# Cached keys stored channel-major, and a new division of state units and gate tiles over the two halves of the samples' attention

## What is computed

```python
def attention_sample(q, k, v, iq, ik, iw, rel_bias, cache_k, cache_v, cache_ik, page_table):
    rows = (page_table[:, :, None] * PAGE_SIZE + jnp.arange(PAGE_SIZE)[None, None, :]).reshape(DB, past)
    ik_all = jnp.concatenate([cache_ik.reshape(-1, IDX_DIM)[rows], ik], axis=1)
    idx = indexer_topk(iq, iw, ik_all, q_pos, n_sel)       # relu(iq . ik), weighed, top 256 of 1025
    ...                                                    # keys and values of the chosen positions
    return sparse_attention(q, k_sel, v_sel, q_pos, idx, rel_bias)

def ssd_recurrent(xs, dt, A, bm, cm, h0):                  # one step for each sample
    h = h * jnp.exp(dtt * A)[..., None, None] + jnp.einsum('bgr,bgrp,bgn->bgrpn', dtt, xt, bt)
    y = jnp.einsum('bgn,bgrpn->bgrp', ct, h)
```

## Time and profile before

| | us |
|---|---|
| median of 3 runs | 1402.03 (1401.03 to 1403.03) |
| the profiled execution, first to last instruction | 1401.1 |
| samples' attention | 354.9 to 498.4 |
| of it key half / softmax stretch / value half / tail | 76.0 / 10.8 / 46.0 / 10.7 |
| busy in the whole span: TensorE / VectorE / ScalarE / GpSimd | 1226.1 / 859.2 / 580.2 / 386.1 |

### The profile page before, as it was taken

How to read it: one execution, slowest core, us unless ns; L and a number is a source line. 1 busy time by engine, 2 the same in 40 slices (tenths; PEclk the granted TensorE clock), 3 DMA queues, 4 the chain that set the end, 5 groups by cost and what they waited for, 6 DMA issues and landing times.

```text
span 1401.1 us, 17183 instructions
## 1 busy us (share of the span) xinstructions
PE 1226.1 (88%) x4958; PEld 747.1 (53%) x4958; DVE 859.2 (61%) x2353; ACT 580.2 (41%) x1545; POOL 386.1 (28%) x510
## 2 busy tenths in 40 slices
PE   7998799999879989999899999877887877878786
PEld 6876477777656677678785553322232222222231
DVE  2055589998762347511248687789956767776543
ACT  1164458887654235300125434433343333333433
POOL 3220012213111200100023445433643334433341
PEclk9999899999999999989999999999999999999999
DMA  6563023324887821233369999999999999999995
GB/s 213 164 210 118 31 95 105 106 91 134 311 290 261 282 106 46 78 112 111 111 255 425 426 425 426 428 426 426 426 428 426 427 426 427 428 426 425 428 421 237
DMA packets 80473, 390.22 MB, mean 279 GB/s; under 512 B 13464, under 2 KB 23224, under 8 KB 44288
## 3 DMA queue, kind: packets, MB, share of 16 engines
q0 software_dynamic: 43104, 287.92, 49.5%
q1 hardware_dynamic: 34144, 92.68, 19.2%
q10 hardware_dynamic: 3136, 8.57, 1.7%
...
## 4 chain that ended last, share of the span: by engine, by line
DMA 25%; PE 16%; issue 3%; DVE 3%; ACT 2%; POOL 1%; POOLq 0%; DVEq 0%
DMA pe_uv<-d_uv,pe_idx 24%; PE pe_acc L1828 8%; PE pq_ps L1767 4%; PE pe_ph L1828 2%; POOL pe_uv L1951 1%; DMA pe_uv<-d_uv,pe_idxs 1%; DVE pe_uv L2090 1%; ACT pe_dg L1895 1%; ACT pe_w L1892 1%; DVE pe_tp L1994 1%; PE pe_ps L1786 0%; DVE pe_tv L1989 0%; ACT pe_gl L1889 0%; PE pe_pss L1786 0%; DVE pe_cand L2000 0%
## 5 line engine op out<-in xcount | busy, mean ns | idle before, releaser
L2090 DVE CUSTOM_DVE_ANT_0 pe_uv<-pe_uv,pe_hnat 128x1024 f32<-128x1024 f32 x264 | 322.8, 1223 | 186.2 <-DMA pe_uv<-d_uv,pe_idx 171.3
L1951 POOL DMA_INDIRECT pe_uv<-d_uv,pe_idx x256 | 271.9, 1062 | 382.5 <-PE pe_ph L1828 177.7
L1828 PE MATMUL pe_ph<-pe_uv,pe_dg 128*128 128x512 f32 x512 | 252.7, 617 | 65.2 <-ACT pe_dg L1895 65.2
L1828 PE MATMUL pe_acc<-pe_uv,pe_dg 128*128 128x512 f32 (+1 forms) x544 | 257.2, 611 | 45.2 <-ACT pe_dg L1895 45.2
L1828 PEld LDWEIGHTS pe_ph<-pe_uv,pe_dg 128*128 128x128 f32 x512 | 86.9, 189 | 230.3 <-ACT pe_dg L1895 167.8
L139 PE MATMUL pi_ps<-xn,pi_w 128*128 128x264 f32 x848 | 203.4, 395 | 3.1 <-DVE xn L350 3.1
L1889 ACT ACTIVATE pe_gl<-pe_a 128x1 f32<-128x1 f32 x264 | 53.4, 202 | 366.6 <-DVE pe_a L2090 366.4
L1828 PEld LDWEIGHTS pe_acc<-pe_uv,pe_dg 128*128 128x128 f32 (+1 forms) x544 | 94.3, 185 | 199.6 <-ACT pe_dg L1895 110.7
L139 PEld LDWEIGHTS pi_ps<-xn,pi_w 128*128 128x128 f32 x848 | 162.1, 195 | 31.3 <-issue 4.4
L1895 ACT ACTIVATE pe_dg<-cst,pe_w 128x128 f32<-128x128 f32 x256 | 102.7, 401 | 8.3
L1892 ACT ACTIVATE pe_w<-pe_gl,pe_gw 128x1 f32<-128x1 f32 x256 | 75.4, 295 | 8.3
...
## 6 DMA issues: line engine op xcount, KB each, us to landing
...
ss_h<-d_state SPq DMA_DIRECT2D x8, 1024.0 KB, 7.5
o_ssm_s<-ss_h SPq DMA_DIRECT2D x8, 1024.0 KB, 9.5
...
paged<-d_ck POOLq DMA_DIRECT2D x40, 128.0 KB, 5.0
paged<-d_cv POOLq DMA_DIRECT2D x32, 128.0 KB, 5.1
```

Source lines behind the costliest of these rows:

```text
L1828: mm = pe.matmul(accs[n][0:m, 4 * half:4 * half + 4, :], lhsT, uv[:, r, D_MODEL + half * 512:D_MODEL + (half + 1) * 512], start=False, sto ...
L1951: pool.indirect_dma_start(uv[:, r, :], None, k.d_uv[:], bass.IndirectOffsetOnAxis(ap=src, axis=0)).then_inc(gathered[r], 16)
L2090: dve.tensor_tensor_reduce(uv[:, r, 0:D_MODEL], uv[:, r, 0:D_MODEL], hnat[:, n, :], 1.0, 0.0, ALU.mult, ALU.add, a[:, r:r + 1]).then_inc(d ...
```

## The change

The host stores the cached keys and indexer keys channel-major: channels on the partitions, positions along the row. An indexer page is then 64 rows of 512 bytes and goes to the upper or the lower 64 partitions, two pages side by side; a key page is as before 128 rows of 1 KB. The transposes and the copies of both stages go, with the tiles `cs_ikt`, `as_kt` and `cs_tr` (`cs_px` is left of it), and the products read `paged` itself. The ring's loads now wait for the products of a visit (`logits`) where they waited for its transposes. In the new listing the changed lines stand some 15 to 27 lines higher.

The work beside the two halves is divided anew: 8 units and 8 gate tiles in the key half (12 and 4 before), 8 units and 5 gate tiles in the value half's steps (4 and 9 before); the two gate tiles in the softmax stretch and the last one remain. SP's queue starts with state and gate weights in turns, and the stores and reloads stand at other visits.

```diff
@@ -48,7 +48,7 @@
 FIRST0 = N_ATT + 1
 GATE0 = FIRST0 + N_Z + N_XBC
-N_LAST, N_KEYS = 16, 4
+N_LAST, N_KEYS = 16, 8
 COLUMNS = "z" * 8 + "x" * 4 + "z" * 2 + "x" * 28 + "z" * 6
@@ -58,7 +58,7 @@
 Q0, K0, V0, IQ0 = 0, 8, 10, 12
 IW_P, DT_P = 64, 96
 WSLOTS, BANKS = 4, 2
-IK_FIRST, IK_SECOND = 36, 50
+IK_FIRST, IK_SECOND, IK_PAIRS = 18, 25, TS * PAGES // 2
 KV_SLOTS, KV_PAGES = 4, 4
@@ -247,11 +247,12 @@
 def load_indexer_pages(eng, k, first, end, loaded):
-    ik = k.paged[:].rearrange("p (a d) -> p a d", d=HD)
+    ik = k.paged[:].rearrange("p (a s) -> p a s", s=PG)
     with eng.Fori(first, end) as i:
-        page = eng.value_load(k.pages[0:1, bass.ds(i, 1)], min_val=0, max_val=k.n_pool - 1)
-        eng.dma_start(ik[:, bass.ds(i, 1), :], k.d_cik[bass.ds(page, 1)].rearrange("a s d -> s a d")
-                      ).then_inc(loaded, 16)
+        for odd in range(2):
+            page = eng.value_load(k.pages[0:1, bass.ds(i * 2 + odd, 1)], min_val=0, max_val=k.n_pool - 1)
+            eng.dma_start(ik[odd * HD:(odd + 1) * HD, bass.ds(i, 1), :],
+                          k.d_cik[bass.ds(page, 1)].rearrange("a d s -> d a s")).then_inc(loaded, 16)
 def project_attention(nc, k):
@@ -535,33 +537,23 @@
                       ).then_inc(spread, 1)
             k.proj.multiply(pe, tail[0])
-            pe.wait_ge(k.ik_loaded, 16 * (TS * PAGES - IK_SECOND + IK_FIRST))
-            pe.wait_ge(k.ik_by_sp, 16 * (IK_SECOND - IK_FIRST))
+            pe.wait_ge(k.ik_loaded, 32 * (IK_PAIRS - IK_SECOND + IK_FIRST))
+            pe.wait_ge(k.ik_by_sp, 32 * (IK_SECOND - IK_FIRST))
             def scores(b):
-                pe.wait_ge(copied, b + 1)
                 for half in range(2):
                     hd = slice(half * HD, half * HD + HD)
-                    pe.matmul(ps[0:TS * IH, half, :], iqd[hd, b, :], ikt[hd, b % 2, :],
+                    pe.matmul(ps[0:TS * IH, half, :], iqd[hd, b, :],
+                              ik[hd, b * (PAGES // 2):(b + 1) * (PAGES // 2), :].rearrange("p a s -> p (a s)"),
                               start=b == 0, stop=b == TS - 1)
                 pe.matmul(ps[0:TS * IH, 2, 0:1], iqd[0:HD, b, :], k.misc[0:HD, TP + b:TP + b + 1],
                           start=b == 0, stop=b == TS - 1).then_inc(scored, 1)
-            for b in range(TS + 1):
-                if b < TS:
-                    if b >= 2:
-                        pe.wait_ge(copied, b - 1)
-                    for j in range(PAGES // 2):
-                        at = b * PAGES + 2 * j
-                        mm = pe.transpose(tr[:, b % 2, j * P:(j + 1) * P],
-                                          ik[:, at:at + 2, :].rearrange("p a d -> p (a d)"), k.ident)
-                    mm.then_inc(turned, 1)
-                if b == 1:
-                    pe.wait_ge(diag, TS)
-                if b:
-                    scores(b - 1)
-                if b == 5:
+            pe.wait_ge(diag, TS)
+            for b in range(TS):
+                scores(b)
+                if b == 4:
                     pe.wait_ge(s_weighed, 2)
                     pe.wait_ge(dA_ready, 1)
@@ -595,17 +587,10 @@
             act.wait_ge(k.steps_loaded, 48)
             act.activation(alog, alog, ACT.Exp).then_inc(alog_ready, 1)
             k.proj.evacuate(act, tail[0])
-            for b in range(TS):
-                act.wait_ge(turned, b + 1)
-                if b >= 2:
-                    act.wait_ge(scored, b - 1)
-                act.activation(ikt[:, b % 2, :], tr[:, b % 2, :], ACT.Copy).then_inc(copied, 1)
-                if b == 1:
-                    act.wait_ge(u_ready, 1)
-                    act.activation(l, u, ACT.Ln).then_inc(log_ready, 1)
-                if b == 4:
-                    act.wait_ge(dA_ready, 1)
-                    act.activation(both[rows, TS:2 * TS], k.dA[rows, NP_:ALL], ACT.Exp).then_inc(both_dA, 1)
+            act.wait_ge(u_ready, 1)
+            act.activation(l, u, ACT.Ln).then_inc(log_ready, 1)
+            act.wait_ge(dA_ready, 1)
+            act.activation(both[rows, TS:2 * TS], k.dA[rows, NP_:ALL], ACT.Exp).then_inc(both_dA, 1)
             act.wait_ge(scored, TS)
             for half in range(2):
@@ -1341,12 +1325,12 @@
...
-        EARLY = 12
+        EARLY = 8
...
@@ -1355,15 +1339,16 @@
         VK = PAGES * TS // GP
-        after = ([[(t - 3) // 3] if t % 3 == 0 and 3 <= t < 3 + 3 * N_KEYS else [] for t in range(VK)]
+        after = ([[t // 2] if t % 2 == 1 else [] for t in range(VK)]
                  + [[N_KEYS, N_KEYS + 1]] + shares(range(N_KEYS + 2, N_LAST - 1), TS))
+        unit_at = {2 * u: u for u in range(EARLY)}
         spans = ((0, 512), (512, 512), (PAST, 1))
         def load(eng, loaded, half, visit):
             if visit < VK + NG:
-                eng.wait_ge(turned, 2 * (visit - NG + 1))
+                eng.wait_ge(logits, visit - NG + 1)
             elif visit >= VK + NG:
                 eng.wait_ge(mixed, visit - VK - NG + 1)
@@ -1388,16 +1373,16 @@
         def _(sp):
             for b in range(ssd.SLOTS):
                 ssd.load(sp, b)
-            store_at = {6 + 2 * b: b for b in range(6)} | {24: 6, 28: 7}
-            load_at = {7 + 2 * i: ssd.SLOTS + i for i in range(TS - ssd.SLOTS)}
+                gates.load(sp, b)
+            store_at = {8: 0, 12: 1, 16: 2, 19: 3, 24: 4, 28: 5, 31: 6}
+            load_at = {9: 3, 13: 4, 17: 5, 20: 6, 25: 7}
             for visit in range(NG, 2 * VK):
                 load(sp, by_sp, 0, visit)
                 if visit in store_at:
                     ssd.store(sp, store_at[visit])
                 if visit in load_at:
                     ssd.load(sp, load_at[visit])
-                if visit - NG < gates.SLOTS:
-                    gates.load(sp, visit - NG)
+            ssd.store(sp, TS - 1)
             ssd.all_stored(sp)
         @block.gpsimd
@@ -1416,37 +1401,25 @@
             def products(visit):
                 page = visit // 2
-                pe.wait_ge(copied, 2 * visit + 2)
+                arrived(pe, visit)
                 for j in range(2):
                     for i in range(GP):
                         rows = slice(32 * i, 32 * i + 32)
                         mm = pe.matmul(pl[rows, page // 4, page % 4 * P:(page % 4 + 1) * P],
                                        qd[:, 2 * i + visit % 2, j, :],
-                                       kt[:, (2 * visit + i // 2) % 4, (2 * (i % 2) + j) * P:(2 * (i % 2) + j + 1) * P],
+                                       kv[:, visit % NG, i, j * P:(j + 1) * P],
                                        start=False, stop=False, tile_position=(0, 32 * i))
                 mm.then_inc(logits, 1)
-            for n in range(4 * PAGES + 2):
-                if n < 4 * PAGES:
-                    visit = n // 2
-                    if n % 2 == 0:
-                        arrived(pe, visit)
-                    if n >= 2:
-                        pe.wait_ge(copied, n - 1)
-                    for i in range(2):
-                        for j in range(2):
-                            mm = pe.transpose(tr[:, n % 2, (2 * i + j) * P:(2 * i + j + 1) * P],
-                                              kv[:, visit % NG, 2 * (n % 2) + i, j * P:(j + 1) * P], k.ident)
-                    mm.then_inc(turned, 1)
-                if n % 2 == 0 and 0 <= n // 2 - 1 < EARLY:
-                    ssd.spread_c(pe, n // 2 - 1)
-                if n % 2 == 1 and n >= 3:
-                    products(n // 2 - 1)
-                if n % 2 == 1 and n // 2 < VK:
-                    for g in after[n // 2]:
-                        gates.multiply(pe, g)
-                if n % 2 == 1 and n // 2 < EARLY:
-                    ssd.spread_b(pe, n // 2)
+            ssd.spread_b(pe, 0)
+            for visit in range(VK):
+                products(visit)
+                if visit in unit_at:
+                    ssd.spread_c(pe, unit_at[visit])
+                for g in after[visit]:
+                    gates.multiply(pe, g)
+                if visit + 1 in unit_at:
+                    ssd.spread_b(pe, unit_at[visit + 1])
             for b in range(TS):
                 for j in range(2):
                     pe.matmul(pl[b // 2 * 32:b // 2 * 32 + 32, 2, 0:1], qd[:, b, j, :], k.att[:, K0 + j, TP + b:TP + b + 1],
@@ -1495,16 +1468,11 @@
         @block.scalar
         def _(act):
-            for n in range(4 * PAGES):
-                act.wait_ge(turned, n + 1)
-                if n >= 4:
-                    act.wait_ge(logits, n // 2 - 1)
-                act.activation(kt[:, n % 4, :], tr[:, n % 2, :], ACT.Copy).then_inc(copied, 1)
-                if n % 2 == 1 and n // 2 < EARLY:
-                    ssd.fade(act, n // 2)
-                if n % 2 == 0 and n:
-                    for g in after[n // 2 - 1]:
-                        gates.evacuate(act, g)
+            for visit in range(VK):
+                if visit in unit_at:
+                    ssd.fade(act, unit_at[visit])
```

(6 more changed lines are left out.)

26 lines of the change are left out of this document (13 added, 13 removed).

## The result

The changed kernel takes 1389.7 us (median of four runs, 1388.98 to 1390.46), beside 1402.5 for the kernel before on the same chip: a ratio of 0.9904, 95% interval 0.9884 to 0.9925, or 12.8 us less. The forecast was 1385.0 with a range of 1376 to 1394. The profiled execution spans 1388.9 us, 12.2 less than that of before.

A forecast was written before the change was run, and what follows sets the result against it. TensorE was taken to set the pace of both halves, with DMA close behind. 14.0 + 7.0 - 5.0 + 1.0 = 17.0 us off the profiled 1401.1 gives 1384.1, plus 0.9 for the median: 1385.0 us, range 1376 to 1394.

The forecast's parts named there:

- The chain of waits first: Whole kernel: it ends in the expert part, which the change leaves alone, so earlier savings or losses arrive at the end unchanged.
- Key half: First stretch of the samples' attention: eight TensorE rounds of 6.63 us plus waits, ending at 417 against 430.95, 14.0 us less.
- SP's queue: Page loads queued behind reloads waiting for stores: costed at nothing, cover thin; as a rival, slower, 1405 us, 4%.
- DMA, drained by 468: Samples' attention transfers: 1 to 2 MB lag drains in the softmax stretch; last value page lands near 468.
- DMA sets the pace: Rival, 24%: engines at 0.9 of their time put the last page at 475.5 instead of 467; 8.5 us dearer, 1393.
- Value half: Value stretch of the samples' attention: 39 us against 46.0 before, 7.0 us less, ending at 467.
- two waits for the DVE's reads: Value half: in two steps without a gate a spread waits for the unit before, 2 us twice on 34.8 us.
- Softmax stretch: Between key and value halves: 10.8 us as before, starting the value half at 427.8.
- Tail: After the last value product: DVE copies 2.8 us later, lower clock +2.8, gate gives 0.6 back; 10.7 to 15.7, +5.0 us.
- Choice of keys: Stage before the samples' attention: 32 transposes and 8 copies go, 1.0 us less (0.3 to 1.9).
- Expert part: End of the kernel, untouched by the change: as long as before; another length would break the first step.

The follow-up runs named there:

- its second run: Changed kernel plus 4 us of useless DVE copies at the end of the samples' attention, meant to delay scan and merge: 1389.6 us, ratio 0.9914.
- four slots: Changed kernel with four slots for states instead of three, so no reload waits for its slot's store: 1385.7 us, ratio 0.9900 to the kernel before.
- states in the gap: Changed kernel with four state slots and states 6 and 7 loaded ahead of the pages of value visit 20: 1383.2 us, ratio 0.9857.
- small stores: Changed kernel writing back only 2 of each state's 16 chunks, the rest of the output left unwritten: 1383.3 us, ratio 0.9869 to the kernel before.
- last gate first: Changed kernel with the last gate tile ahead of TensorE's wait for the output copies: 1389.6 us, ratio 0.9902 to the kernel before.
- last unit early: Changed kernel with the last state unit's spreads ahead of the last two value visits and its fade ahead of gate 14's sigmoid: 1391.6 us, ratio 0.9910.

## Why the prediction was right, and where it missed

**The chain of waits first; later stages pass the gain on.** Only half right. The stages behind kept their work but not their length. TensorE's work in the merge is the same, its clock is not; 30 us of it before, and the stretches that answer to them after:

```profile
578.50:593.50 15.00, 11.85 (x51) 7.58 (x50) 5.46 (x11) 3.46 (x5) 4.24 (x6) 1.00 0.37 134
593.50:608.50 15.00, 14.28 (x38) 9.26 (x37) 4.35 (x10) 0.00 (x0) 0.00 (x0) 0.66 0.18 46
```

```profile
569.40:584.40 15.00, 11.84 (x43) 8.14 (x42) 4.37 (x7) 2.61 (x4) 4.24 (x6) 0.89 0.29 105
584.40:599.40 15.00, 14.28 (x60) 10.56 (x60) 5.20 (x12) 0.00 (x0) 0.00 (x0) 1.00 0.36 105
```

The second stretches begin 95 us behind the scan's start. The engine is busy for 14.28 us in both, with 38 records in the one and 60 in the other. In the first stretches it is the changed kernel that has part of its time at the lower level. Scan and merge took 155.9 to 157.6 us in four traces (changed, its second run, four slots, states in the gap) and 160.7 to 161.8 in the ten others, before among them, most of these edits of the changed kernel. So the 4.9 us are not the work of transposes or division. What decides between the lengths stays open; the delay that should have tested it delayed nothing.

**Key half, -14.0 forecast, -13.1 measured** (-10.5 to -15.5 by other traces of the same code). The size held, the reason only in part. The forecast took TensorE's work as the bound before, since it was busy for 62.1 of 76.0 us. The runs show that the half was paced by the units and their states: taking the transposes out of it made it no shorter, and the new division without that gave 7.2 us. It came out near since the forecast did not subtract 20.8 us, but laid out the new round and found no wait in it. The round was 5.92 us for 6.63, mostly as the products came at 0.58 apart and not 0.8, a figure that no row of before had: 5.7 us better. The waits for pages (5.7 us in four, for the 3 us I had allowed), the first round at the lower clock (364.37 less 355.60 is 8.8 us for 5.9) and the last visits at it took that back.

**SP's queue, costed at nothing; DMA, drained by 468.** This step failed. The last pair of value pages was read at 469.7, near the 468 forecast, but the pages before them came late all along, which a sum of bytes up to the last one does not show. The small stores price it: 5.6 us in the key half, 4.0 in the value half. The rival "DMA sets the pace" named the right mechanism, though the engines came to a share of 0.97 and not 0.9 in the key half, and its last page at 475.5 came at 469.7. That its price (8.5 us) is close to those 9.6 proves nothing: its own 126 us, from a start near 354, end at 480, or near 473 by my estimate if the last two stores (2.1 MB) come behind; 475.5 is neither.

SP's holds were not free either. SP waited 16.5 us for stores in four waits. The prediction named the visits whose pages are held, 10 and 14, and called the cover of 1 to 2 us thin: TensorE waited 0.47 us at visit 10 and 2.61 at visit 14. The hold of the reload of state 7 was looked at only for its unit; it held visit 26, with 2.82 us. That is 5.9 of the 13.1 us of waits for pages. But without the holds (four slots) 10.9 us of such waits are left at other visits, so most of the price is the transfers' and not the queue's.

**Value half, -7.0 forecast, -2.4 measured.** 39 us forecast, 43.4 measured. The work held (34.8 us forecast, 36.05 us busy). The 4 us for two waits for the DVE's reads did not come: no such wait stands in the trace. In their place there were 7.4 us of waits for pages, which had been put at nothing. So the total hides two misses of opposite sign.

**Softmax stretch, 0 forecast, +1.0.** Its first gate ran at the lower clock (5.51 us for 3.83). The gate ahead of it, at 409.52, ran at the full clock, and TensorE had been busy since 406.45. With last gate first, last unit early and small stores the stretch takes 10.9 and the gate 3.83. It does not go by the waits of the key half: last unit early had 3.9 us of waits for pages and the full clock, states in the gap 3.0 and the lower one. What decides stays open.

**Tail, +5.0 forecast, +7.2 measured.** The two parts were right in kind. The copies started 5.5 us behind the last value product where 2.8 were forecast: the cause is not the reload of state 7 but that the last spread stands behind the last product, and the last fade behind the sigmoid of gate 14. The lower clock cost 0.5 + 1.9 us (forecast 2.8). The Trainium skill, TensorE: Matmul & The Clock Gate, section "HAM oscillation — how this bites in real kernels", warns of bursts that run cold behind a wait; the trace agrees, with 5.75 us behind 7.30 us idle and 3.73 with the gate moved ahead.

**Choice of keys, -1.0 forecast, -0.9 measured** at the last score, counted from `dA` as the forecast had it. `dA` itself came 0.4 us later, and 1.2 us more arose behind the score, in the clock of the next block, which the forecast did not have.

**Expert part.** 1.8 us longer in this trace; in the other traces it takes 740.6 to 742.1 us, before 741.3. I take it for the spread of single executions.

In sum the forecast was 4.8 us too low: value half 4.6, tail 2.2, softmax 1.0, key half 0.9 and the expert part 1.8 against it; scan and merge 4.9 and the start 0.8 for it. That it fell within the range is owed to a clock stretch that it did not know of: without the 4.9 us the time would have been 1394.6, just above the range's 1394 (an estimate).
